# One more tile of lag for the shared expert's products, and the first modulation products as four column tiles

## The reference

```python
cond = jax.nn.silu(c)
mod = (cond @ ada_w[l] + ada_b[l])[:, None, :]
sh1, sc1, g1, sh2, sc2, g2 = jnp.split(mod, 6, axis=-1)
h = (_rms(x) * norm1_g[l] * (1.0 + sc1) + sh1).astype(dt)
mixed = _hybrid_mixer(h, w_in[l], ...)
x = x + g1 * mixed
h = (_rms(x) * norm2_g[l] * (1.0 + sc2) + sh2).astype(dt)
# in _moe_ffn: top-8 of 64 experts for each token, then per block of rows of one expert
hid = jax.nn.silu(xb @ w1[e]) * (xb @ w3[e])
ob = (hid @ w2[e]) * rw[:, None]
# and for every token
shared = (jax.nn.silu(h @ ws1) * (h @ ws3)) @ ws2
x = x + g2 * (y[:t] + shared)
```

## Time and profile before

| | before |
|---|---|
| median of 3 runs | 2583.17 us (2578.26 to 2585.08) |
| profiled execution, device time | 2582.63 us |
| its span | 2580.9 us |
| PE busy | 2439.3 us (95%) |
| DVE, ACT, POOL busy | 1181.7, 485.5, 641.7 us |
| mean granted TensorE clock | 0.979 of full |

### The profile page before, as it was taken

One profiled execution on the slowest core, in us unless ns is written; L12 is line 12 of the kernel. 1 busy time (PEld: TensorE's weight loads), 2 busy tenths in 40 slices (PEclk: granted clock), 3 DMA queues, 4 the chain that ended last, 5 costly groups with the idle time before them and its releaser, 6 DMA issues.

```text
span 2580.9 us, 32556 instructions
## 1 busy us (share of the span) xinstructions
PE 2439.3 (95%) x8542; PEld 1187.8 (46%) x8543; DVE 1181.7 (46%) x2728; ACT 485.5 (19%) x894; POOL 641.7 (25%) x653
## 2 busy tenths in 40 slices
PE   6999999999999999999999998899998998997985
PEld 3444444555545565555444553344443443443432
DVE  3376222666646656763355665232333334233331
ACT  3311001444431233332111222000000000000000
POOL 0000000000031100001111336454444444534441
PEclk9999999999999999999999999999998999998998
DMA  9111335342362422223334126788799799979883
GB/s 270 54 39 46 77 78 149 107 124 98 113 170 70 98 60 74 78 90 119 110 110 131 50 74 248 224 286 267 223 321 304 234 308 377 337 244 379 286 274 78
DMA packets 122931, 437.48 MB, mean 170 GB/s; under 512 B 22204, under 2 KB 24460, under 8 KB 97120
## 3 DMA queue, kind: packets, MB, share of 16 engines
q1 hardware_dynamic: 78208, 306.91, 34.3%
q0 software_dynamic: 44640, 129.49, 19.3%
HBM read 369.72 MB, written 73.93 MB: 172 GB/s over the span
## 4 chain that ended last, share of the span: by engine, by line
PE 81%; DVE 7%; another core or an unknown queue 4%; issue 3%; DMA 2%; ACT 1%; POOL 1%; ACTq 0%; SPq 0%; DVEq 0%; POOLq 0%
PE psum L928 21%; PE psum L1384 17%; PE psum L1434 8%; PE psum L992 7%; PE psum L1238 6%; PE psum L1255 3%; PE psum L1389 3%; PE psum L1195 2%; PE psum L1440 2%; PE psum L1063 2%; PE psum L1073 2%; PE psum L1082 1%; PE psum L1299 1%; PE psum L1478 1%
## 5 line engine op out<-in xcount | busy, mean ns | idle before, releaser
L928 PE MATMUL psum<-mem 128*128 128x512 f32 x1536 | 691.5, 596 | 2.0 <-ACT mem L1566 2.0
L1384 PE MATMUL psum<-mem 128*128 x1008 | 456.6, 609 | 17.6 <-issue 13.4
L928 PEld LDWEIGHTS psum<-mem 128*128 128x128 f32 x1536 | 280.9, 191 | 296.3 <-issue 295.3
L777 POOL DMA_INDIRECT mem<-h_d,idx x312 | 317.0, 1016 | 389.3 <-DVE idx L2609 269.7
L1384 PEld LDWEIGHTS psum<-mem 128*128 128x128 f32 x1008 | 195.2, 196 | 278.4 <-issue 277.8
L2587 DVE TENSOR_TENSOR mem<-mem,psum 128x256 f32<-128x256 f32 x93 | 39.1, 421 | 489.0 <-ACT mem L1838 438.2
L1434 PE MATMUL psum<-mem 128*128 128x512 f32 x504 | 246.2, 621 | 3.7 <-issue 3.5
L992 PE MATMUL psum<-mem 128*128 128x512 f32 x448 | 192.8, 592 | 0.0
L782 POOL DMA_INDIRECT out_x<-mem,put x93 | 142.0, 1527 | 136.7 <-issue 136.0
L1838 ACT ACTIVATE mem<-psum 128x256 f32<-128x256 f32 x93 | 35.6, 384 | 718.3 <-PE psum L1384 390.1
L1238 PE MATMUL psum<-mem 128*128 128x512 f32 x384 | 165.0, 592 | 0.0
(11 more groups left out here) (398 smaller groups left out, 2524.8 us busy)
## 6 DMA issues: line engine op xcount, KB each, us to landing
mem<-in_exp_w SPq DMA_DIRECT2D x201, 1024.0 KB
mem<-in_w_in SPq DMA_DIRECT2D x16, 2048.0 KB, 14.1
proj_d<-mem SPq DMA_DIRECT2D x104, 256.0 KB, 2.1
mem<-in_ada_w POOLq DMA_DIRECT2D x16, 1024.0 KB, 6.2
mem<-proj_d POOLq DMA_DIRECT2D x56, 256.0 KB, 3.0
mem<-proj_d POOLq DMA_DIRECT2D x20, 512.0 KB, 5.5
mem<-in_ada_w SPq DMA_DIRECT2D x4, 2048.0 KB, 19.6
mem<-in_w_branch SPq DMA_DIRECT2D x3, 2048.0 KB, 8.0
```

Of the source, the lines that this page charges most:

```text
L777: g.indirect_dma_start(x[:, 2 * P * n:2 * P * (n + 1)], None, h2_q, bass.IndirectOffsetOnAxis(ap=idx[:, p, j, n:n + 1], axis=0), bounds_ch ...
L928: mm = t.matmul(bank(unit_bank(u)), l, r, start=(k == 0), stop=(k == KD - 1))
L1384: return t.matmul(bank(4 + j), xgT[r][:, k, P * j:P * (j + 1)], up_piece(h, r, k), start=(k == 0), stop=(k == KD - 1))
```

## The change

Two parts.

- **Modulation.** `ada_products` uses four column tiles of 32 (steps k mod 4) in one bank in place of two of 64. Same number of instructions, same copy and column sum.
- **Shared expert.** Its lag behind the loop grows by one tile: turn and down run for tile i-5, up for i-4 (for i = 4 to 6). x2 gets a sixth buffer. `route_turn(i)` waits for one `shared_out` fewer. In the tail up, turn and down of tile 3 and up of tile 4 are added, and the list work's matmuls stand between other shared products. DVE's and ACT's orders follow. SP's load of slot 2 waits for the last up product (s_H = 8) in place of the last down product.

```diff
--- before.py
+++ after.py
@@ -168,7 +168,7 @@
         xin = [view(12288 + 1024 * j, D) for j in range(2)]
         g1b, a2b, b2b = (view(at, D) for at in (25600, 15360, 16384))
         g2b = view(10368, D)
-        x2 = [view(at, D) for at in (18432, 19456, 25600, 26624, 14336)]
+        x2 = [view(at, D) for at in (18432, 19456, 25600, 14336, 26624)] + [sb("x2e", [P, D])[:, :]]
         h2 = [view(20480 + 1024 * j, D) for j in range(2)]
         rwt = view(23680, KD, NE)
         shw2 = [view(17408, D), view(22528, D)]
@@ -543,23 +543,25 @@
 
             def store_shared(i):
                 sp.wait_ge(s_ya, i + 1)
-                sp.dma_start(y_out[i * P:(i + 1) * P, :], x2[i % 5]).then_inc(s_ys[i % 2], 16)
+                sp.dma_start(y_out[i * P:(i + 1) * P, :], x2[i % 6]).then_inc(s_ys[i % 2], 16)
 
             for i in range(NT):
                 sp.wait_ge(s_h2, i + 1)
                 sp.dma_start(h2_d[i * P:(i + 1) * P, :], h2[i % 2]).then_inc(s_so[i % 2], 16)
-                if i >= 4:
-                    store_shared(i - 4)
+                if i >= 5:
+                    store_shared(i - 5)
             sp.wait_ge(s_mx, NT)
             for b in range(2):
                 load_up(b, b)
                 load_down(b, b)
             sp.wait_ge(e_clear, 1)
             load_up(3, 3)
-            for i in range(4, NT):
+            for i in range(3, 6):
                 store_shared(i)
-            sp.wait_ge(s_sO, NT)
+            sp.wait_ge(s_H, NT)
             load_up(2, 2)
+            for i in range(6, NT):
+                store_shared(i)
             sp.wait_ge(s_tab, 1)
             with sp.Fori(1, NI // 4) as it:
                 with sp.If(tokens(sp, 4 * it - 2) > 0):
@@ -886,8 +888,8 @@
                     pe.wait_ge(s_part, j - 1)
                 w = slot(("ada", j))
                 for k in range(KD):
-                    mm = t.matmul(psum[64 * (k % 2):64 * (k % 2) + 64, 4 + j % 2, :], condp[:, k, :], w[:, k, :],
-                                  start=(k < 2), stop=(k >= KD - 2))
+                    mm = t.matmul(psum[32 * (k % 4):32 * (k % 4) + 32, 4 + j % 2, :], condp[:, k, 0:32], w[:, k, :],
+                                  start=(k < 4), stop=(k >= KD - 4))
                 mm.then_inc(s_adm, 1)
 
             def ada_columns(j):
@@ -1260,8 +1262,8 @@
             def route_turn(i):
 
                 pe.wait_ge(s_h2, i + 1)
-                if i >= 4:
-                    pe.wait_ge(s_ya, i - 3)
+                if i >= 5:
+                    pe.wait_ge(s_ya, i - 4)
                 for k in range(KD):
                     mm = t.transpose(psum[:, 4 + k // 4, (k % 4) * P:(k % 4 + 1) * P], h2[i % 2][:, k * P:(k + 1) * P], ident[:, :])
                 mm.then_inc(s_h2t, 1)
@@ -1311,8 +1313,8 @@
                 pe.wait_ge(s_hc, i + 1)
                 if i == 0:
                     pe.wait_ge(s_wo, 3)
-                if i <= 3:
-                    pe.wait_ge(s_h2c, i + 4)
+                if i <= 2:
+                    pe.wait_ge(s_h2c, i + 5)
                 else:
                     pe.wait_ge(s_h2c, NT)
                 if 1 <= i < NT - 1:
@@ -1325,8 +1327,8 @@
 
             for i in range(NT):
                 out_half(i, 0)
-                if i >= 4:
-                    shared_turn(i - 4)
+                if i >= 5:
+                    shared_turn(i - 5)
                 if i >= 1:
                     route_turn(i - 1)
                 out_half(i, 1)
@@ -1334,27 +1336,31 @@
                     rank(i - 2)
                 if i >= 1:
                     route(i - 1)
-                if i >= 4:
-                    shared_down(i - 4)
-                if i >= 3:
-                    shared_up(i - 3)
+                if i >= 5:
+                    shared_down(i - 5)
+                if i >= 4 and i < 7:
+                    shared_up(i - 4)
             route_turn(7)
             route(7)
             rank(6)
-            shared_up(5)
-            shared_turn(4)
-            shared_down(4)
+            shared_up(3)
+            shared_turn(3)
+            shared_down(3)
             rank(7)
-            shared_turn(5)
             pe.wait_ge(s_pm, NT)
             t.matmul(psum[:, 7, 0:NE], ones[:, :], total[1], start=True, stop=True)
             t.matmul(psum[0:NE, 7, NE:NE + 1], total[1], ones[:, 0:1], start=True, stop=True).then_inc(s_cn, 1)
-            shared_up(6)
+            shared_up(4)
+            shared_up(5)
             pe.wait_ge(s_tp, 1)
             t.matmul(psum[0:NE, 7, 128:129], strict[0:NE, 0:NE], over[:, 0:1], start=True, stop=True).then_inc(s_ts, 1)
-            shared_down(5)
+            shared_turn(4)
+            shared_down(4)
+            shared_up(6)
             pe.wait_ge(s_tp, 2)
             t.matmul(psum[:, 7, 256:256 + 3 * NV], ones[0:NE, :], items.rearrange("p a b -> p (a b)"), start=True, stop=True).then_inc(s_ts, 1)
+            shared_turn(5)
+            shared_down(5)
             shared_up(7)
             pe.wait_ge(s_tp, 3)
             t.transpose(psum[0:NE, 6, 0:P], absent, ident[:, :]).then_inc(s_ts, 1)
@@ -1779,7 +1785,7 @@
                 act.wait_ge(s_x2, i + 1)
                 if i >= 1:
                     act.wait_ge(s_sq, i)
-                s.activation(h2[i % 2], x2[i % 5], ACT.Square, accum_out=stat[:, 32 + i:33 + i]).then_inc(s_sq, 1)
+                s.activation(h2[i % 2], x2[i % 6], ACT.Square, accum_out=stat[:, 32 + i:33 + i]).then_inc(s_sq, 1)
 
             def rows_copy(i):
                 act.wait_ge(s_h2t, i + 1)
@@ -1804,21 +1810,24 @@
                 s.activation(shT.rearrange("p k n -> p (k n)"), psum[:, 3, 0:FF], ACT.Copy).then_inc(s_hc, 1)
 
             for i in range(NT):
-                if i >= 4:
-                    shared_copy(i - 4)
+                if i >= 5:
+                    shared_copy(i - 5)
                 if i >= 1:
                     rows_copy(i - 1)
                 squares(i)
                 if i >= 1:
                     scores(i - 1)
-                if i >= 3:
-                    shared_silu(i - 3)
+                if i >= 4 and i < 7:
+                    shared_silu(i - 4)
             rows_copy(7)
             scores(7)
+            shared_silu(3)
+            shared_copy(3)
+            shared_silu(4)
             shared_silu(5)
             shared_copy(4)
+            shared_silu(6)
             shared_copy(5)
-            shared_silu(6)
             shared_silu(7)
             shared_copy(6)
             shared_copy(7)
@@ -2332,14 +2341,14 @@
 
             def residual(i):
 
-                y, z = x2[i % 5], h2[i % 2]
+                y, z = x2[i % 6], h2[i % 2]
                 dve.wait_ge(s_mx, i + 1)
                 dve.wait_ge(s_xi[i % 2], 16 * (i // 2 + 1))
                 if i >= 2:
                     dve.wait_ge(s_so[i % 2], 16 * (i // 2))
                     dve.wait_ge(s_h2t, i - 1)
-                if i >= 5:
-                    dve.wait_ge(s_ys[(i - 5) % 2], 16 * ((i - 5) // 2 + 1))
+                if i >= 6:
+                    dve.wait_ge(s_ys[(i - 6) % 2], 16 * ((i - 6) // 2 + 1))
                 v.tensor_tensor(y, banks(2 * (i == 1), 2), xin[i % 2], ALU.add).then_inc(s_x2, 1)
                 if i >= 2:
                     slots(i - 2)
@@ -2409,9 +2418,11 @@
 
             def shared_out(i):
                 dve.wait_ge(s_sO, i + 1)
+                if i == 5:
+                    dve.wait_ge(s_ys[1], 16 * 2)
                 if i == 6:
                     dve.wait_ge(s_ys[0], 16 * 3)
-                v.tensor_tensor(x2[i % 5], x2[i % 5], banks(2 if i == NT - 1 else 4, 2), ALU.add).then_inc(s_ya, 1)
+                v.tensor_tensor(x2[i % 6], x2[i % 6], banks(2 if i == NT - 1 else 4, 2), ALU.add).then_inc(s_ya, 1)
 
             def shared_hidden(i):
                 dve.wait_ge(s_si, i + 1)
@@ -2491,23 +2502,26 @@
 
             for i in range(NT):
                 residual(i)
-                if i >= 4:
-                    shared_out(i - 4)
+                if i >= 5:
+                    shared_out(i - 5)
                 if i >= 1:
                     choose(i - 1)
-                if i >= 3:
-                    shared_hidden(i - 3)
+                if i >= 4 and i < 7:
+                    shared_hidden(i - 4)
             slots(6)
             choose(7)
+            shared_hidden(3)
+            slots(7)
+            shared_out(3)
+            count_items()
+            shared_hidden(4)
+            list_items()
             shared_hidden(5)
-            slots(7)
+            absent_tokens()
             shared_out(4)
-            count_items()
-            list_items()
+            table()
             shared_hidden(6)
-            absent_tokens()
             shared_out(5)
-            table()
             dve.wait_ge(s_l4, 64)
             some = lambda x, e, n, c: x[:, bass.ds(e, n), c:c + 1].rearrange("p j o -> p (j o)")
             by_item = first4[:, :, :, 0:1].rearrange("p g (e j) c -> p e j (g c)", j=NT)
```

## The result

| | before | after |
|---|---|---|
| median | 2583.81 us (8 runs, 2578.26 to 2586.37) | 2589.36 us (8 runs, 2586.17 to 2597.22) |
| ratio after / before | | 1.0034, 95% interval 1.0022 to 1.0046 |
| profiled execution, its span | 2582.63, 2580.9 us | 2586.17, 2584.5 us |
| E, end of the last shared product | 1588.2 | 1595.3 |

The kernel became 5.5 us slower by the medians, 0.2% of its time. As in the prediction, r7 is the start of DVE's add in `residual(7)`, E the end of the last shared product, and the tail is what lies between them; a hole is a stretch in which PE stands idle. The profiled execution of after is the fastest of its eight, so what it shows behind E is weaker evidence than what it shows before.

What follows compares the result with a forecast made beforehand. PE bounds the kernel up to E, the end of the shared products, on which the expert ramp hangs. Modulation -4.1, loop and tail +11.5, clock +1.7 gave +9.1 on 2582.6: 2591.7, with the median's 0.5 2592, range 2582 to 2599.

Steps and rivals of the forecast that it cites:

- Modulation, -4.1: First modulation products: 1.9 us each on four tiles; projection starts at 47.9, when w_in lands, instead of 52.04: -4.1 us.
- Rival 3: Modulation products: four tiles run no faster than two, nothing gained, and the tail's +13.2 stands: 2595.8 us; chance 0.13.
- The router loop, -10.2: Loop before r7: 10.6 us of PE work leaves, periods shorten by 7.6 and 2.6, r7 comes 10.2 us sooner.
- The tail, 78.7: From r7 to E: 78.7 us instead of 57.0, with 10.6 more work, about 11 waiting, new idles 4.7 and 4.1.
- Clock, +1.7: Tail: half clock after PE idles of 2.0 us or more; the second new idle slows down(3), +1.7 (bounds 0 and 3.4).
- Sum at E: Modulation -4.1, loop and tail together +11.5, clock +1.7: +9.1 us.
- Behind E, 0: Expert stage's ramp is paced by E and keeps its shape: 0, bounds -6.9 and +2.
- a sign against it: Ramp from E to the third item: shorter than before by more than 3 us would show the forecast wrong.
- rival 2: Before the third item: the 6.9 us idle may vanish with slot 2's weights in before E, 2584.8 us; chance 0.22.
- The gathers: First expert rows: gathered rows there 8.9 us after DVE's first tokens, as before, at 1594.7, before E, costing nothing.
- Rival 1: Expert ramp follows the list chain, not E: stage starts 6.8 us sooner, kernel ends at 2571.7 us; chance 0.10.

Runs made afterwards that it cites:

- The dummy products: Changed kernel with five added, unused products in PE's idle ahead of `route_turn(7)`: 2526.97 us, ratio 1.0041 against the kernel before.
- the kernel without the lag: Kernel before with four column tiles and early ACT token copies, slot 2's load moved to s_H = 8: 2513.64 us, 0.9985; without that move 2508.43 us, 0.9967.
- the version with early copies: Kernel before with four column tiles and ACT's token copies waiting for the up products, no longer lag: 2508.43 us, ratio 0.9967 against the kernel before.

## Why the prediction was right, step by step

The forecast was 2592 in 2582 to 2599. It came out at 2589.4. The sum was +9.1 us and the medians moved by 5.5: the waits came where they were laid out, the second of them much shorter, and the sum is 3.6 us too high. By the profiles 2.0 of the miss lie at E and 3.2 in the ramp behind it; the profile of after, the fastest of its eight, has +3.6 in all.

- **Modulation, -4.1.** Right: 1.92 us for each later product (1.9 forecast), projection at 47.90 (47.9), then 4.0 us in the kernel that has this part alone. To hit 47.90 to the tenth was luck: in the eleven profiled kernels with the four tiles the projection starts between 47.46 and 49.45, mostly as the w_in block lands. The first product fell from 5.19 to 3.64 instead of to 3.4, which the landing of w_in hides. Rival 3 is out. The price it gave the lag alone, 13.2, was 12.7 by the medians. The Trainium skill, TensorEngine Tiling, Theoretical Speedup, gives up to 4x for 32 columns; from two to four tiles the trace shows 1.86 to 1.90 times (3.58 and 3.65 to 1.92). Four waves of 0.43 are 1.7 of the 1.92, so a drain at the change of tiling has 0.2 us at most.
- **The router loop, -10.2.** Right. The first two periods after tile 3 came out as 17.1 and 24.7, as forecast. With the lag alone the loop from the first `residual` to r7 is 146.2 us instead of 156.4 in the kernel before on such a chip. In the first comparison r7 came 1.2 us sooner still, and this stands already at the first `residual` (1369.43 against 1374.78, -5.35 where the projection gives -4.1), ahead of the changed part of the loop. It is within what executions differ by: with the four tiles the first `residual` starts anywhere from 1368.83 to 1371.12.
- **The tail, 78.7.** Right in place and size: 4.64 of idle for 4.7, DVE's `shared_out(2)` named, 79.7 in all with the clock's part.
- **Clock, +1.7.** The mechanism was right and its place was not. The prediction put the half clock of the first idle in waits behind it and charged the second. In the trace the first idle's half clock stretched up(3) to 8.97, and this used up the second idle, 1.25 of 4.1 us, so that down(3) ran at full clock. Up(3) ended 3.2 us later than laid out, the turn behind it only 0.4. The price was 0.4 instead of 1.7, inside the bounds. The dummy products show the second half of the argument: with the first idle filled the second is 3.72, and down(3) takes 5.18, 1.5 us too long, as the prediction had it. Its rule, half clock after an idle of 2.0 us or more, held in the trace of before but is too narrow: down(3) took 5.17 behind idles of 1.11, 0.70 and 0.47, and 32 up instructions took 15.70 behind 1.71 and 1.12.
- **Sum at E.** -4.1 + 11.5 + 1.7 is +9.1. In the first comparison E moved by 7.1: 1.3 less from r7 and 0.7 less from the tail. Between the profiles of chips 0 and 15 it moved by 9.0, but 1.05 of that is the later w_in block, so this near hit is in part luck.
- **Behind E, 0.** Right on the other chips (third item at E + 28.6 before and E + 28.5 after, span +8.6 for 9.0). In the first comparison the ramp to the third item became 3.2 us shorter, just beyond the 3 us that the prediction named as a sign against it: 2.0 from the wait of 6.90, now 4.87, and 1.0 from the transposes, at E + 14.1 instead of E + 15.1. The kernel before has E + 14.1 too on chip 0, so that 1.0 need not be the change's. The 2.0 are a part of rival 2, not its 6.9. Their cause stays open, since the wait is not there at all on the other chips, in either kernel. The Trainium skill, Runtime: NRT & Kernel Launch, Instruction fetch mechanics, names a fetch behind a taken branch as a cause of such stalls; the same instructions ran without this wait on other chips, so that rule alone does not give it.
- **The gathers.** A term that was missing. Rows were forecast at 1590.6 (1594.7, less the 4.1 of the modulation) and turned at 1593.5: 10.9 us behind the first gather instead of 7.4. Slot 2's load, issued at 1586.45, is in flight beside them; that it makes rows late is shown in the kernel without the lag, and in this one 1.1 us of it at least (10.8 to 9.6 with the load put back). E at 1595.3 covered it. The prediction asked of this load only whether it helps the third item.
- **Rival 1** (the ramp follows the lists, not E) is out: the copies began at E + 0.1, and only an edit that takes their wait for s_sO away lets them start sooner. The edit is worth 2.6 to 4.5 us with the lag. Without it the ratios of the modulation alone and of the version with early copies differ by 0.15%, some 4 us, with overlapping intervals.

Why a lag loses: the loop gave back nearly the work taken out of it (10.2 of 10.6 us), and the tail had to take that work in places where the next engine's answer was not there yet. With the holes filled the lag costs some 4 us, with them open 12.7. Taking the copies off the end of the shared products gained in all three pairs of kernels, by 2.6 to 5 us, though each pair's intervals overlap.

## What to carry to other kernels

In this kernel work moved from a full loop into its tail came back not quite one for one. Before such a move, look first for what then waits for the end of the tail, and whether that wait is needed. When an order is written out by hand, lay it out from a fixed point and price each hole twice, once for its length and once for the clock behind it, then ask whether the slowed work lies in front of another hole. A load that is issued sooner may not be free where small gathers are on their way.

## What the hardware showed that was not expected

**The same kernel differs behind E by 67 us.** Up to E the profiles of the kernel before agree within 0.1 us; the rest is 992.7 us in the first comparison and 925.8 on chip 0. The medians on chips 0, 6 and 15 agree within 1.1 us. Which chip the first comparison ran on is not known, so that it is the chip, and not another condition of those runs, is likely but not shown. Waits by engine and line (us in total, times, longest us) of the kernel before in the first comparison, then of after:

```profile
ACT mem L1838 <- remote: 178.4, 17, 16.1
```

```profile
ACT mem L1847 <- remote: 149.7, 13, 17.0
```

ACT's silu of the up products waits up to 17 us for something that the profile only calls remote. On chips 0 and 15 the same table has no such row, in the kernel before and in the changed one. What it is stays open, and so does whether the 2 us found at the third item belong to it.

**The half clock moves with the holes.** In the tail it followed idles of 3.72 and 4.64 us, once three small ones in a row (1.11, 0.70 and 0.47, before the down product of 5.17) and once 1.71 and 1.12 (before 15.70 for 32 instructions), but not the 1.25 and 0.47 ahead of down(3) in after. At the first expert products it followed 4.79 (8.82 for 16), while behind 1.90 these ran at full clock (7.13) and the next 16 took 10.20, behind 1.32 and 1.25. Behind one idle or row of small ones it cost 1.5 to 1.9 us in most cases, but 3.1 on those 16, and behind the 4.64 it lay on `route(7)` (1.7) and up(3) (1.9). Filling one hole with dummy products moved the drop to the next one and gained nothing.
